# Two-layer streaming encoder: a third PSUM bank for turned probabilities, modulation turned by transposes, a beta product on two column halves, output weights loaded ahead of modulation weights

## What is computed

```python
def modulate(c, mod_w, mod_b):                     # c: 9 condition vectors (1 prompt, 8 samples)
    mod = jnp.dot(jax.nn.silu(c), mod_w) + mod_b   # (9, 3072)
    shift, scale, gate = jnp.split(mod, 3, axis=-1)

# even layer: RG-LRU branch and sliding-window attention, one output projection
hmod = rms_norm(x, norm_pre) * (1.0 + scale) + shift
u = jnp.dot(hmod, w_in)
p = exp(s - mx); p = p / (sum(p) + exp(sink - mx)); o = p @ v    # 8 heads, window of 256 keys
x = x + gate * rms_norm(jnp.dot(concat(y_a, y_b), w_out), norm_post)

# odd layer: gated DeltaNet on the same tokens
qkv, z, b, a = split(jnp.dot(hmod, w_in))          # b and a: 8 columns each
beta = sigmoid(b); g = -exp(a_log) * softplus(a + dt_bias)
x = x + gate * rms_norm(jnp.dot(gated_delta_rule(...) , w_out), norm_post)
```

## Time and profile before

| | before |
|---|---|
| median of 3 runs | 1619.75 us (1617.47 to 1621.44) |
| the profiled execution's own time | 1619.96 us |
| its span, first to last instruction | 1618.2 us |
| PE busy | 1506.6 us, 93% of the span |
| PE weight load busy | 928.3 us |
| DVE busy | 731.2 us, 45% |
| ACT busy | 409.3 us, 25% |
| POOL busy | 175.6 us, 11% |
| mean granted TensorE clock | 0.966 of 2.4 GHz |
| moved by DMA | 100.51 MB |

### The profile page before, as it was taken

The page is one execution under the profiler, slowest core; times in us unless marked ns, Lnnn a source line. Parts: engine busy times, 40 slices in busy tenths (PEclk is TensorE's granted clock), DMA queues, the critical chain, the costliest instruction groups (busy, mean ns, idle before and its releaser), DMA issues.

```text
span 1618.2 us, 32776 instructions
## 1 busy us (share of the span) xinstructions
PE 1506.6 (93%) x14320; PEld 928.3 (57%) x14320; DVE 731.2 (45%) x1650; ACT 409.3 (25%) x1036; POOL 175.6 (11%) x366
## 2 busy tenths in 40 slices
PE   4997999999989996899989999999999999999997
PEld 2454555566643444456656666666666766666533
DVE  4205443343322126274563745737457474562251
ACT  5003333344410023311321313222132221221220
POOL 1000000000000011012020210202102021020020
PEclk9898999999999997999999999999999999999999
DMA  8511003000133113011111110201102111030041
GB/s 322 243 32 30 30 30 103 1 1 1 58 149 147 61 59 124 14 56 32 38 39 37 55 30 28 57 30 54 31 28 56 31 55 32 1 141 2 29 156 65
DMA packets 53011, 100.51 MB, mean 62 GB/s; under 512 B 34458, under 2 KB 37346, under 8 KB 50290
## 3 DMA queue, kind: packets, MB, share of 16 engines
q1 hardware_dynamic: 52868, 98.41, 18.0%
HBM read 83.54 MB, written 14.86 MB: 61 GB/s over the span
## 4 chain that ended last, share of the span: by engine, by line
PE 56%; DVE 4%; issue 2%; ACT 1%; POOL 0%; POOLq 0%; DVEq 0%; ACTq 0%
PE psum L689 54%; PE psum L692 2%; DVE mem L1609 1%; DVE mem L2083 0%; DVE mem L2021 0%; DVE mem L1898 0%; DVE mem L1867 0%; DVE mem L1793 0%; ACT mem L1357 0%; DVE mem L1785 0%; DVE mem L2138 0%; DVE mem L1787 0%; DVE mem L1884 0%; ACT mem L1384 0%; ACT mem L1389 0%
## 5 line engine op out<-in xcount | busy, mean ns | idle before, releaser
L689 PE MATMUL psum<-mem 32*32 32x32 f32 (+8 forms) x13728 | 1435.3, 287 | 74.8 <-issue 31.6
L689 PEld LDWEIGHTS psum<-mem 32*32 32x32 f32 (+5 forms) x13728 | 857.0, 136 | 623.0 <-issue 282.6
L1867 DVE SCALAR_TENSOR_TENSOR mem<-mem 128x384 f32<-128x384 f32 (+1 forms) x216 | 138.0, 639 | 2.4
L692 PE MATMUL psum<-mem 128*128 128x128 f32 (+1 forms) x592 | 92.7, 294 | 28.4 <-ACT mem L1244 17.3
L692 PEld LDWEIGHTS psum<-mem 128*128 128x128 f32 (+1 forms) x592 | 73.7, 152 | 57.7 <-issue 38.8
L1785 DVE SCALAR_TENSOR_TENSOR mem<-psum,mem 128x512 f32<-128x512 f32 x13 | 9.8, 750 | 132.7 <-POOL mem L573 125.5
L1458 ACT ACTIVATE mem<-psum 128x288 f32<-128x288 f32 (+1 forms) x40 | 15.8, 396 | 172.1 <-PE psum L689 172.1
L1357 ACT ACTIVATE mem<-psum 128x512 f32<-128x512 f32 x26 | 15.3, 593 | 159.2 <-PE psum L689 157.5
L1408 ACT ACTIVATE mem<-psum 128x384 f32<-128x384 f32 x48 | 23.4, 490 | 109.6 <-PE psum L689 109.6
L1334 ACT ACTIVATE mem<-mem 128x256 f32<-128x256 f32 x72 | 35.5, 494 | 47.8 <-DVE mem L1746 47.8
L569 POOL TENSOR_TENSOR mem<-mem 128x1 f32<-128x1 f32 x18 | 5.4, 298 | 381.0 <-ACT mem L1357 381.0
(11 more groups left out here) (186 smaller groups left out, 933.3 us busy)
## 6 DMA issues: line engine op xcount, KB each, us to landing
mem<-modw SPq DMA_DIRECT2D x12, 2048.0 KB, 10.1
mem<-w SPq DMA_DIRECT2D x44, 512.0 KB, 3.5
x_dram<-mem SPq DMA_DIRECT2D x1, 4608.0 KB, 13.3
mem<-row_dram SPq DMA_DIRECT2D x8, 576.0 KB, 3.8
mem<-x_dram SPq DMA_DIRECT2D x9, 512.0 KB, 3.6
y<-mem SPq DMA_DIRECT2D x9, 512.0 KB, 3.1
mem<-gs SPq DMA_DIRECT2D x8, 512.0 KB, 4.4
ss<-mem SPq DMA_DIRECT2D x8, 512.0 KB, 2.6
```

The lines of the kernel that those rows point to most:

```text
L689: return pe.matmul(*a, **k)
L692: return pe.transpose(out, in_, ident[0:n, 0:n])
L1867: x = dve.scalar_tensor_tensor(cvm, U1[:, m, lo + j:hi + j], w, cvm, ALU.mult, ALU.add)
```

## The change

It moves turn 2 of attention ahead of weigh 0 and gives it bank 5. It turns the modulation by 16 plain transposes into banks 4 to 7 and has DVE sum the four partition groups in four reductions. The beta product is split into four token ranges (384, 384, 192, 192 columns); two at a time share a bank, one on partitions 0 to 39 and one on 64 to 103, their matmuls alternating. SP waits for the output weights to land before it issues the first two modulation loads.

```diff
+TURN_BANK = (6, 7, 5, 6)
+BA_PARTS = ((5, 0, 0, NC), (5, 64, NC, 2 * NC), (6, 0, 2 * NC, 5 * NC // 2), (6, 64, 5 * NC // 2, TOK))
...
             sp.dma_start(wout[:, 0:wo_d], I["wout"][0, :, 0:wo_d]).then_inc(sem("wout_in"), 16)
+            sp.wait_ge(sem("wout_in"), 32)
             mod_loads(1, 0)
             mod_loads(1, 1)
...
-            def mod_turn(bank):
+            def mod_turn():
                 for j in range(16):
-                    i = mm(B(bank)[:, 9 * j:9 * j + 9], modrow[:, j * P:(j + 1) * P], fold,
-                           start=True, stop=True)
+                    i = tr(B(4 + j // 4)[:, (j % 4) * P:(j % 4 + 1) * P], modrow[:, j * P:(j + 1) * P])
...
             pe.wait_ge(sem("mod_ev"), 4)
-            mod_turn(0)
+            pe.wait_ge(sem("n_ev"), NT)
+            mod_turn()
...
                 def turn(u):
                     pe.wait_ge(sem("p_norm"), 4 * t + u + 1)
-                    if not first or u >= 2:
-                        pe.wait_ge(sem("pt_ev"), 4 * t + u - 1)
+                    if u == 3:
+                        pe.wait_ge(sem("pt_ev"), 4 * t + 1)
+                    elif not first:
+                        pe.wait_ge(sem("pt_ev"), 4 * t)
...
-                            i = tr(B(6 + u % 2)[:, (2 * a + w) * P:(2 * a + w + 1) * P],
+                            i = tr(B(TURN_BANK[u])[:, (2 * a + w) * P:(2 * a + w + 1) * P],
...
                 turn(0)
+                turn(1)
+                turn(2)
+                weigh(0)
+                turn(3)
                 for u in range(1, 4):
-                    turn(u)
-                    weigh(u - 1)
-                weigh(3)
+                    weigh(u)
...
-            for n in range(3):
+            for pair in (BA_PARTS[0:2], BA_PARTS[2:4]):
                 for k in range(KT):
-                    i = mm(B(5 + n)[0:40, 0:NC], wba[:, k], HT[:, k, n * NC:(n + 1) * NC],
-                           start=(k == 0), stop=(k == KT - 1))
+                    for bank, r, a, b in pair:
+                        i = mm(B(bank)[r:r + 40, 0:b - a], wba[:, k], HT[:, k, a:b],
+                               start=(k == 0), stop=(k == KT - 1))
...
-            for n in range(3):
-                c.mark(act.activation(Z[0:H, 0, n * NC:(n + 1) * NC], B(5 + n)[0:H, 0:NC], ACT.Copy, scale=-1.0))
-                c.mark(act.activation(Z[0:H, 1, n * NC:(n + 1) * NC], B(5 + n)[32:40, 0:NC], ACT.Copy))
+            for bank, r, a, b in BA_PARTS:
+                c.mark(act.activation(Z[0:H, 0, a:b], B(bank)[r:r + H, 0:b - a], ACT.Copy, scale=-1.0))
+                c.mark(act.activation(Z[0:H, 1, a:b], B(bank)[r + 32:r + 40, 0:b - a], ACT.Copy))
...
-                c.mark(dve.tensor_copy(modT.rearrange("p a b -> p (a b)"), B(bank)[:, 0:144]))
+                for q in range(4):
+                    c.mark(dve.tensor_reduce(
+                        modT[:, 4 * q:4 * q + 4],
+                        B(4 + q).rearrange("p (j g r) -> p j r g", g=4, r=32)[:, :, 0:9],
+                        AX.X, ALU.add))
```

More of the change, by code:

```diff
@@ L908, in _ @@
             pe.wait_ge(sem("mod_ev"), 12)
-            mod_turn(6)
+            mod_turn()
             for w in range(2):
@@ L1342, in att @@
                         wait(act, sem("pv_mm"), 4 * t + u - 1)
-                    act.activation(PT[:, u % 2].rearrange("p a t -> p (a t)"), B(6 + u % 2), ACT.Copy
+                    act.activation(PT[:, u % 2].rearrange("p a t -> p (a t)"), B(TURN_BANK[u]), ACT.Copy
                                    ).then_inc(sem("pt_ev"), 1)
@@ L1578, in mod_chunk, with mod_columns @@
                                   ).then_inc(sem("mod_ev"), 1)
-            def mod_columns(l, bank):
+            def mod_columns(l):
                 dve.wait_ge(sem("mod_tr"), l + 1)
-                c.mark(dve.tensor_copy(modT.rearrange("p a b -> p (a b)"), B(bank)[:, 0:144]))
+                for q in range(4):
[3 more added lines that the diff above has]
+                        AX.X, ALU.add))
                 c.sync()
@@ L1628, in _ @@
                 mod_chunk(0, n, n)
-            mod_columns(0, 0)
+            mod_columns(0)
             dve.wait_ge(sem("n_ev"), NT)
@@ L1808, in _ @@
             dve.wait_ge(sem("x1_done"), NT)
-            mod_columns(1, 6)
+            mod_columns(1)
             mod_gate(1, 0, 0, "gate_ev")
```

## The result

The changed kernel takes 1596.43 us (median of 4 runs, 1593.05 to 1599.43) against 1620.18 (4 runs): ratio of changed to before 0.9855, 95% interval 0.9831 to 0.9879. Forecast were 1600.7 us and a range of 1595 to 1609. The same kernel run again later with others gave 1599.98 (4 runs, 1597.74 to 1604.72), ratio 0.9886, interval 0.9868 to 0.9904. The later sets ran on chips 1, 2 and 14, where the kernel before had medians of 1619.47, 1619.37 and 1621.05. The profiled execution took 1596.74 us, its span is 1595.0.

What follows compares the result with a forecast made beforehand. PE's work and waits were taken to bound the kernel. Terms of 4.35 + 1.4 + 1.2 + 1.5 + 3.5 + 7.3 = 19.25 us came off 1619.96, giving 1600.7 us, range 1595 to 1609.

Steps and rivals of the forecast that it cites:

- Attention: Attention blocks: turn 2 moved into the idle before weigh 0 gains 0.59 us a block, 4.1 us in blocks 0 to 6.
- with the same small wait as before: Attention: weigh 1 and copy 3 come earlier, so weigh 3 starts 0.59 us earlier, its small wait unchanged.
- Output weights, the clock behind them, block 8: Blocks 7 and 8: weights landing in 9.8 us gain 1.4, less half clock after the wait 1.2, block 8's idle 0.25.
- Layer 0's turning: Layer 0's modulation: 16 transposes for 32 nine-column instructions save 2.2 us, DVE's four reductions add 0.7; sum 1.5.
- I leave that in the range: After layer 0's turning: PE staying at full clock could bring up to 1.8 us more, not counted in the sum.
- Layer 1's turning: Layer 1's modulation: transposes at half clock save 3.0 us, faster gates 0.5; sum 3.5 us.
- 0.5 of the possible 1.5: Layer 1's gates: full clock throughout would save 1.5 us; 0.5 was taken.
- Beta product: Layer 1's beta product: halves side by side save 7.7 us, ACT's two extra evictions cost 0.4; sum 7.3.
- 1 (halves not side by side): Beta product: column halves don't run side by side, 7.7 us come back, 1608.4 us; chance 0.12.
- 2 (transposes leave the clock at half): Both turnings: gates and layer 0's start gain only what is counted, 1.2 us less, 1601.9 us; chance 0.08.
- 3 (weights land no sooner): Output weights: the queue served them first anyway, so their gain and the clock's go, 1603.3 us; chance 0.12.
- 4: Attention: slower, as turn 2 waits for DVE's third pair and holds weigh 0; 1625 us; chance 0.02.

Runs made afterwards that it cites:

- the identity run: The changed kernel with the modulation's 16 transposes made as ordinary matmuls with the 128x128 identity (32 instructions of 128 columns): 1611.26 us, one run.

## Why the prediction was right

**The sign and the range** held since the large terms (attention, turnings, beta product) were PE work on PE's own path, priced by a row of the same instruction. One term, the output weights, came true by luck. Point by point:

- *Attention*, 4.1 us for blocks 0 to 6: measured 3.6, 0.52 a block for 0.59. The step that was off is "with the same small wait as before", and behind it lies a misread row. The prediction has weigh 1 end at 439.05 in the kernel before. What ended there was turn 3:

```profile
438.46 0.66 PE L692 MATMUL psum<-mem 128*128 128x128 f32 x4
```

The row of copy 3 at 439.15 in the earlier trace rows says the same, as it names the transposes of line 692. So before, copy 3 waited for turn 3, and in the changed kernel it waits for weigh 1 (line 692 there is the matmul). Weigh 1's last matmul ended at 430.77, the copy started at 430.87, and PE's idle before weigh 3 grew from 0.10 to 0.32 us. Block 7's gain did go into the wait for the weights, as said.

- *Output weights, the clock behind them, block 8*, 2.85 us: measured 3.06 and 3.05. Landing at 9.8 us and a wait near 2.4 were forecast, 9.8 and 2.31 came. This is luck. The step that failed is that 11.2 us was the price of "4 MB queued behind them": fifteen of the sixteen steps had come after 10.05 us before as well, and the last was late behind an instruction packet, as in four of the twelve profiles with the wait. The clock still fell behind the wait, but for 3.4 us instead of 6.8, and `out(0, 0)` took 15.70 for 16.87: 1.2, the middle figure taken. It hangs on the same luck in part: with the wait in place and a late landing it was at half for 6.8 us in two profiles and for 3.4 in two.
- *Layer 0's turning*, 1.5 us: measured 1.75; the transposes took 1.94 for 2.1, the reductions 0.95 for 1.0. What failed is "I leave that in the range". From there to attention, 2.4 us more were gained. In eleven profiles with transposes this stage took 237.15 to 238.4 us, in the two with 9-column matmuls 239.6 and 240.0, with the identity 239.5. So 1.2 or more goes with the transposes: in and behind the turning the clock was at half for 6.8 us with 9 columns, for 3.4 in seven of the eleven and not at all in four. The other 1.2 is a stretch near 130 us that was at half clock for 13.7 us in some profiles and 6.8 in others. That the change has no part in this one is not shown.
- *Layer 1's turning*, 3.5 us: measured 5.2 and 3.7. The turning took 3.5 for 3.9. The gates, 5.2 before, took 3.6 us in the first profile, all at full clock, and 4.9 in the second. So the term "0.5 of the possible 1.5" lies between the two that were measured, 1.6 and 0.3. Over the eleven profiles with transposes turning and gates took 6.8 to 8.4 us, 7.6 in the mean, against 12.1: 4.5 us.
- *Beta product*, 7.7 less 0.4: measured 8.5 and 7.8 less 0.4. At full clock it is 8.0 us for 7.9. ACT's 192-column evictions took 0.32 for 0.35.
- *Nothing given back later*: no stage grew by what these lost. The first profile has +1.7 and -0.8 us in the last two, the second 0 and +4.5, and both go with the time at half clock.

**Rivals.** 1 (halves not side by side) fell: one group costs 15.7, two alternating 8.0 at full clock. 2 (transposes leave the clock at half) fell twice, by 588.40 to 595.40 in the profile after and by the identity run. In five of the eleven profiles with transposes, though, the clock rose only 1.8 to 2.6 us into the gates. By the Trainium skill's rule (TensorE: Matmul & The Clock Gate, Part 4) the sum would have been 1.2 less; the trace disagrees (0.54 in the stretch of transposes, 1.00 right behind it). 3 (weights land no sooner), given 0.12, is what the traces support: fifteen of sixteen steps came no later without the wait than with it, give or take a few tenths. 4 did not occur: DVE's third pair was ready about 1.1 us before turn 2 (427.0 and 428.1).

The Trainium skill's figure for column tiles (TensorE: Matmul & The Clock Gate, Part 3; 1.6 times for two as an estimate from its 2.38 for three) is below what was measured here: 15.7 / 8.0 = 2.0.

The median of all eight runs lies 2 us below the forecast, the first four 4 us. That the sum is so near is also luck: the turnings and the beta product gave more than their terms and attention less, and unchanged code varies by more than the difference.

## What to carry to other kernels

An idle that an in-order engine spends waiting for another's copy is filled by the next independent step, if it has a bank of its own; after that, look for the buffer that the copy waits for. Two matmuls of 40 columns on partitions 0 and 64 ran side by side at twice the speed when they alternated; one group's eight products after the other's overlapped only in the last two products at each boundary. A late transfer is better issued sooner (here 4.1 us) than protected from the ones behind it (here nothing that the traces show). When a load lands late, look at the steps of its semaphore and at what else its last packets met, before the loads behind it get the blame. Judge an edit of a few us by its own stage, since unchanged stages of the same program vary by more.

## What the runs showed of the hardware that was not expected

- 7 us of 9-column matmuls, PE busy all the time, did not bring TensorE from 1.2 to 2.4 GHz, in two profiles (10.0 and 12.3 us at half in turning and gates). With transposes or 128-column matmuls it was at half for 2.9 to 3.4 us there in seven profiles of twelve and for 5.2 to 6.1 in five. So turning by transposes gave more in what follows (1.2 us or more in layer 0, 0.3 to 1.6 in the gates) than a count of instructions tells.
- 936 us of unchanged code took 934.3 to 944.8 us in 14 profiles. The time at half clock in this stage went from 30.7 to 53.6 us. The two move together loosely (correlation 0.73; 944.8 came with 41.2, 944.7 with 53.6, 934.3 with 37.1), so the clock is likely a part of it, and what else is stays open.
- Column groups in sequence still overlapped, in the last four instructions of a range: 12.6 us at full clock where one group took 15.7.
- A 16 KB instruction packet of 0.95 us that met the last packet of a 3 MB load made its last step 1.2 to 1.4 us later than the other fifteen, in six of fourteen profiles.
